# A decoder step with a mixture of experts: two expert weight loads issued earlier, and 16 matrix products without a reader ahead of the first expert block

## The reference

```python
merged = g_a * (y_a @ w_pa) + g_b * (y_b @ w_pb) + g_c * (y_c @ w_pc)
x = layer_norm(ALPHA * x + (1 + g1) * (merged @ w_o), ln1_g, ln1_b)
h2 = x * (1 + sc2) + sh2
...
scores = jax.nn.sigmoid(h @ w_router)          # group-limited top 2 of scores + bias
for e in range(N_EXPERTS):
    he = jax.nn.silu(h @ w_e_gate[e]) * (h @ w_e_up[e])
    y = y + gate[..., e:e + 1] * (he @ w_e_down[e])
x = layer_norm(ALPHA * x + (1 + g2) * y, ln2_g, ln2_b)
```

## Time and profile before

| | |
|---|---|
| median of 3 runs | 1046.58 us (1044.06 to 1046.66) |
| profiled execution | 1057.31 us, its span 1055.4 us |
| PE busy | 998.1 us (95%), 9475 matmul records |
| DVE, ACT, POOL busy | 548.5, 198.9, 254.2 us |
| granted TensorE clock, mean | 0.97 |
| HBM read, written | 201.12 MB, 16.92 MB |

### The profile page before, as it was taken

How to read it: one execution, slowest core, us unless ns; L and a number is a source line. 1 busy time by engine, 2 the same in 40 slices (tenths; PEclk the granted TensorE clock), 3 DMA queues, 4 the chain that set the end, 5 groups by cost and what they waited for, 6 DMA issues and landing times. The chain is left out here.

```text
span 1055.4 us, 23402 instructions
## 1 busy us (share of the span) xinstructions
PE 998.1 (95%) x9475; PEld 719.8 (68%) x9475; DVE 548.5 (52%) x1381; ACT 198.9 (19%) x474; POOL 254.2 (24%) x284
## 2 busy tenths in 40 slices
PE   5999999999999999899999999977999999999995
PEld 4677777557776767576777764554776777677763
DVE  1131899984457888976456815687233121011137
ACT  1110012213222323232111110111111111111104
POOL 0010002824121223123335620000211212422123
PEclk8998999999999999899999999976999999999998
DMA  9964742653605215014072336242799999899995
GB/s 307 308 139 114 240 161 82 217 206 122 238 21 164 77 31 195 20 46 126 11 191 69 120 98 271 70 189 101 306 423 416 357 410 396 347 383 396 389 277 113
DMA packets 94003, 214.98 MB, mean 204 GB/s; under 512 B 23572, under 2 KB 48407, under 8 KB 89797
## 3 DMA queue, kind: packets, MB, share of 16 engines
q1 hardware_dynamic: 78388, 186.20, 49.5%
q0 software_dynamic: 6672, 19.67, 6.2%
q10 hardware_dynamic: 8841, 7.64, 2.6%
HBM read 201.12 MB, written 16.92 MB: 207 GB/s over the span
## 5 line engine op out<-in xcount | busy, mean ns | idle before, releaser
L2120 PE MATMUL banks<-arena 128*128 128x288 f32 (+6 forms) x1774 | 427.6, 396 | 6.3 <-issue 2.5
L2120 PEld LDWEIGHTS banks<-arena 128*128 128x128 f32 (+1 forms) x1774 | 317.1, 191 | 108.9 <-issue 32.4
L2520 PE MATMUL banks<-arena 128*32 128x256 f32 x3136 | 186.7, 384 | 4.1 <-issue 2.9
L2520 PEld LDWEIGHTS banks<-arena 128*32 128x32 f32 x3136 | 131.7, 110 | 48.5 <-issue 8.1
L2048 DVE TENSOR_TENSOR arena<-arena,banks 128x128 f32<-128x128 f32 x49 | 14.1, 288 | 222.7 <-ACT arena L1353 222.5
L2542 PE MATMUL banks<-arena 128*32 128x256 f32 x1568 | 100.2, 379 | 1.5 <-issue 0.8
L1051 POOL DMA_INDIRECT expert_rows<-arena,ints x44 | 43.0, 977 | 196.9 <-ACT arena L1364 192.8
L993 POOL TENSOR_SCALAR arena<-arena 128x288 f32<-128x288 f32 x46 | 44.9, 975 | 168.2 <-ACT arena L1275 102.1
L1430 DVE SCALAR_TENSOR_TENSOR arena<-arena 128x512 f32<-128x512 f32 x120 | 82.0, 743 | 0.0
L2542 PEld LDWEIGHTS banks<-arena 128*32 128x32 f32 x1568 | 61.5, 109 | 21.7 <-issue 6.4
L2134 PE MATMUL banks<-arena 128*128 128x288 f32 x256 | 69.9, 431 | 2.7 <-DVEq L1448 2.7
(11 more groups left out here) (321 smaller groups left out, 998.4 us busy)
## 6 DMA issues: line engine op xcount, KB each, us to landing
arena<-in_w_e_gate SPq DMA_DIRECT2D x16, 2048.0 KB
arena<-in_w_e_up SPq DMA_DIRECT2D x16, 2048.0 KB
arena<-in_w_e_down SPq DMA_DIRECT2D x16, 2048.0 KB
arena<-in_w_ada SPq DMA_DIRECT2D x8, 2048.0 KB, 10.3
arena<-in_w_in SPq DMA_DIRECT2D x8, 2048.0 KB, 9.7
arena<-in_w_ada SPq DMA_DIRECT2D x8, 1024.0 KB, 11.6
arena<-in_x_prompt SPq DMA_DIRECT2D x8, 512.0 KB, 7.0
arena<-in_w_in SPq DMA_DIRECT2D x14, 256.0 KB, 8.2
```

Of the source, the lines that this page charges most:

```text
L2120: last = pe.matmul(out, a, b, start=k == 0, stop=k == len(pairs_) - 1)
L2520: last = pe.matmul(out, HG[:, g % 2, k, a:a + BLK], both_weights(i, k, c), start=k == 0, stop=k == KT - 1)
```

## The change

It does two things. First, the masks OHL, GE, OHH and the small HIS move from A_XR to a place of their own at the end of the arena (A_HOTS = A_SUMS, the arena 736 words a partition longer), so that slot 6 no longer waits for weights_up but for x1_up at 5, the last reading of R. The up weights of turn 1 are issued right behind the down weights of turn 1, in the step t == 1 of the w_o stage. Second, `unread` puts products of the identity with 256 constant columns, whose result nobody reads, into a free PSUM bank: 3 ahead of ("h2T", 4, 0), one ahead of ("cum", 3), one ahead of ("near", 3), 9 ahead of the transposes of the first gathered rows and 2 behind them.

```diff
--- before.py
+++ after.py
@@ -110,7 +110,8 @@
 A_GT = A_PT + 1024
 A_SM = A_GT + 4 * HALF + 70
 A_SUMS = A_SM + 164
-A_END = A_SUMS + 2 * 512
+A_END = A_SUMS + 2 * NT * (TS + 2 * NHI + 2)
+A_HOTS = A_SUMS
 
 A_X = A_UN
 A_WSN = A_MG
@@ -445,8 +446,8 @@
     TOTAL, NMEAN, SQUARES, RSTD2, EPSN = sm(28, 5), sm(33, 5), sm(62, 5), sm(67, 5), sm(38, 1)
     RCON = V(r0 + 1119, R_ALL)
 
-    OHL, GE, OHH = V(A_XR, 2 * NT, TS), V(A_XR + 2 * NT * TS, 2 * NT, NHI + 1), V(A_XR + 2 * NT * (TS + NHI + 1), 2 * NT, NHI)
-    SAB, HIS = V(r0 + 811, 2 * NT), V(A_XR + 2 * NT * (TS + 2 * NHI + 1), 2 * NT)
+    OHL, GE, OHH = V(A_HOTS, 2 * NT, TS), V(A_HOTS + 2 * NT * TS, 2 * NT, NHI + 1), V(A_HOTS + 2 * NT * (TS + NHI + 1), 2 * NT, NHI)
+    SAB, HIS = V(r0 + 811, 2 * NT), V(A_HOTS + 2 * NT * (TS + 2 * NHI + 1), 2 * NT)
     CMP, CMP2 = V(A_H2T, NE, NE), V(A_H2T + 256, NE, NE)
     KEY, NUM, BASE, CAP, ORD = (V(A_H2T + 512 + 16 * k, NE) for k in range(5))
 
@@ -739,7 +740,7 @@
     def room(eng, n):
 
         if n < RING:
-            eng.wait_ge(ev("weights_up"), 1)
+            eng.wait_ge(ev("x1_up"), NT)
         else:
             j, y = divmod(n - RING, 3)
             eng.wait_ge(ev("dn_full" if y == 2 else "hid_full"), FIRST[j + 1])
@@ -852,6 +853,7 @@
                 expert_weights(sp, 0, 0, 0)
                 expert_weights(sp, 0, 1, 1)
                 expert_down(sp, 1, 5)
+                expert_weights(sp, 1, 1, 4)
             if t >= 1:
                 sp.wait_ge(ev("h2_ready"), 2 * t)
                 sp.dma_start(h2_d[(t - 1) * P:t * P, :], H2[:, (t - 1) % 2, :]).then_inc(ev(f"h2_out{(t - 1) % 2}"), 16)
@@ -861,7 +863,6 @@
         sp.wait_ge(ev("h2_ready"), 2 * NT)
         sp.dma_start(h2_d[SEQ:NTOK, :], H2[0:NS, 0, :]).then_inc(ev("h2_out0"), 16)
         sp.wait_ge(ev("rows_gathered0"), 16)
-        expert_weights(sp, 1, 1, 4)
         sp.wait_ge(ev("order_known"), 1)
         for i in range(2, NE):
             e = sp.value_load(ints[0:1, I_ORD + TURNS[i]:I_ORD + TURNS[i] + 1], min_val=0, max_val=NE - 1)
@@ -2158,11 +2159,21 @@
                         last = pe.matmul(ps[NS * z:NS * z + NS, 0:256], MG[:, k, SEQ:NTOK], w[k][:, 256 * z:256 * z + 256], start=k == 0, stop=k == KT - 1)
             return last
 
+        def unread(times, cols):
+
+            pe.wait_ge(*mm.taken(("wo", 3, 1)))
+            for _ in range(times):
+                pe.matmul(mm.tile(("wo", 3, 1))[:, 0:cols], ident, con[:, 0:cols], start=True, stop=True)
+
+        fillers = {("h2T", 4, 0): (3, 256), ("cum", 3): (1, 256), ("near", 3): (1, 256)}
+
         pe.wait_ge(ev("consts"), 16)
         for key in plan:
             kind = key[0]
             if kind == "tk":
                 continue
+            if key in fillers:
+                unread(*fillers[key])
             if kind == "mod":
                 continue
             if kind == "acc":
@@ -2543,7 +2554,9 @@
                                      start=k == 0, stop=k == NJ - 1)
             last.then_inc(ev("dn_full"), 1)
 
+        unread(9, 256)
         gathered(0, 0, 16)
+        unread(2, 256)
         for b in range(NBLK + 2):
             if b < NBLK:
                 hidden(b)

```

## The result

The kernel after takes 1042.08 us in the median of 12 runs (1036.93 to 1047.35), the kernel before 1047.08 (1044.06 to 1052.73, 12 runs too, the first three of them those shown above). The two medians are 5.0 us apart; the ratio of the two sets of runs is 0.9936 (0.9918 to 0.9955), which is 6.7 us faster, 4.7 to 8.6. The forecast was 1044.1 against 1046.58, a gain of 2.5.

The account below looks back on a forecast made before the run. The prediction took TensorE to bound the expert stage, with DMA just as full, and a half clock at its start. Products 1.3 plus loads 1.2 gave 2.5 us off the median 1046.58: 1044.1, range 1041.0 to 1047.6.

Parts of the forecast that it names:

- the term for the wait ahead of block 11: Expert stage: one load less in the queue removes block 11's 1.69 us wait; 1.7 us, 1.2 for an undisturbed run.
- the up weights of turn 1: Load issued earlier, in the w_o stage: nobody waited for these weights, so by itself it gives nothing.
- the last load come 5.2 to 6.2 us forward: Queue ahead of block 11: one of eight loads gone brings the last 5.2 to 6.2 us forward.
- The one ahead of ("near", 3): Routing: this unread product finds no hole at half clock and moves the gather 0.7 us later.
- The three and the one ahead of ("cum", 3): Routing: these early unread products lie where PE idles or others wait, so they are hidden and cost nothing.
- The nine: Ahead of the first gathered rows' transposes: dense unread products take 5.6 to 6.8 us, and the clock rises during them.
- the net at block 3: First expert blocks: first block 0.95 us late, clock loss won back; net gain 1.3 us in the median run.
- rival three: Ahead of the first block: identity products do not raise the clock, or it falls again; 2.9 us slower, chance 0.07.
- block 27's wait of 1.21 moves along with PE: Expert stage: slots after block 15 fill as PE frees them, so this wait stays and moves with PE.
- rival one: Routing or expert stage: more gain than counted, by either of two branches, time 1041.7 or 1041.0; chance 0.38.
- the early products holding the clock: Routing, a branch of rival one: clock stays up, first block 1.35 us sooner, 4.9 us gained, time 1041.7.
- both waits gone: Blocks 11 and 27, a branch of rival one: no weight waits or late clock fall; 5.6 us gained, time 1041.0.

Follow-up runs that it names:

- e1: The kernel after without all 16 unread products, only the two loads issued earlier: 0.9938 of before, 1043.01 us against 1049.32.
- e5: e1's kernel with the up weights of turn 1 back behind the gather, only the gate weights of turn 2 early: 0.9941 of before.
- e7: The kernel before with only half of turn 2's down weights loaded (1 MB of 2), nothing moved: 0.9943 of before.
- e6: The kernel before with only the up weights of turn 1 issued early, no unread products: 1.0026 of before.
- e3: The kernel before, unchanged, run and profiled again: 0.9996 of before.
- e2: The kernel before plus the 16 unread products, loads not moved: 0.9969 of before.
- e8: The kernel after without the early five unread products (three, one and one); the 9 and the 2 stay: 0.9921 of before.
- e4: The kernel after, unchanged, run and profiled again: 0.9942 of before.
- e9: The kernel after with the two 0.5 MB loads of ln2's rows issued in turn 12 in place of turn 9: 0.9923 of before.
- e12: The kernel after without the early five unread products and with ln2's rows in turn 12: 0.991 of before, 1039.85 us against 1049.35.
- e10: The kernel after without any unread products and with ln2's rows in turn 12: 0.992 of before, 1040.84 us.
- e11: The kernel after without the 9 and the 2 unread products; the early five stay: 0.9953 of before.

## Why the prediction missed

The direction and the places were right, the size was not: 6.7 us came and 2.5 were forecast. The range (1041.0 to 1047.6) held the time, 1042.08.

**The step that failed** is the term for the wait ahead of block 11: "Term: 1.7, bounds 0 and 2.9 [...] I take 1.2 for an undisturbed run." The loads measured 6.5 (e1) and 6.2 (e5). The mechanism was as written: block 11 waits for weights that come late behind a full queue (the landings at e7), one load less takes the wait away (e1, e5), and the up weights of turn 1 give nothing (e6). Two things were mis-sized. The wait came from one profile, 1.69 us; in e3 it is 2.92. And I priced it as idle time alone, with the clock behind it at nothing and no reason given. In e3 the clock fell after it, and again after the wait ahead of block 27, 1.7 us each. Falls near 27 are in the profiles of e2, e3, e6 and e7 and in none of the nine with the gate weights early.

The runs agree. In the mean, time at half clock is 62 us in 29 runs of before and 57 in 11 of e1, which is worth 2.7 of the 5.6 us between the mean times; for e5 it is 2.9 of 6.5. The rest, 2.9 and 3.6, is the size of the larger wait (2.92 in e3), but the timed runs do not say where it lies. Shaving 1.7 to 1.2 because profiled executions are slow had no row behind it and went the wrong way: 6.1 of the 10.7 us that this execution lay over the median were the slow blocks. The sum also had the last load come 5.2 to 6.2 us forward; from issue to landing it gained 3.1 to 4.9, still enough. Why the clock fell after a wait in some executions and not in the first profile of before is not settled; the length of the wait does not decide it.

**The unread products** went as worked out where each step can be checked. The one ahead of ("near", 3) delays the gather at half clock (0.7 forecast; the nine start 0.68 later in after than in e8). The three and the one ahead of ("cum", 3) are hidden, and none of the five holds the clock. The nine took 6.9 us (5.6 to 6.8 forecast), the first block came 1.35 late (0.95), blocks 0 and 1 gave back 2.8 (2.97), and the net at block 3 was 1.4 to 1.5 (1.3). In the mean of the runs, too: time at half clock is 56.8 us in e1 and 51.5 in e4, worth 2.7, of which the late first block takes back 1.35. But a net of 1.3 is below what the timed runs can tell.

The clock stayed up through the eight transposes and the copies: in after, e2, e4, e8, e9 and e12 blocks 0 and 1 follow them in 7.12 us, and rival three did not happen. The Trainium skill (TensorE: Matmul & The Clock Gate, Part 4) has it that transposes do not count as busy for the clock. No fall followed them here (0.9 us of them in after), and no run tests the rule by itself.

**What I did not see** is the wait ahead of block 27. The prediction had it that "block 27's wait of 1.21 moves along with PE". The 1.21 was a low value to begin with, as e3 shows (2.29, same kernel). It was 2.85 and 2.66 in the two profiles of after, 2.08 with the loads alone, and from e1 to after about 1 of the 1.4 us that the products had won at block 3 was gone at block 48. That is no rule: e8, 4.7 us ahead of e1 at block 3, waited 2.22 and kept 4.6. e9 shows that the wait is for weights, since moving 1 MB out of their way removes it; the landings say the same, block 27 starting 0.09 us after the last landing of turn 9's up weights wherever there is a wait. Why it was longer in after is not shown; the loads of that stretch are issued at nearly the same distances behind PE. Nor is it shown why the products add 3.2 us to before and nothing measurable to the loads: without the wait (e9 and e10) the timed runs show nothing either, and the intervals are wide enough for one small gain in both places.

**The slow blocks** 28 to 32 of the profiled before were read by nobody in the forecast, and they were no part of the kernel; a comparison of the two first profiles alone would have credited the change with 11.9 us.

The chances: faster by over 0.3% had 0.38, which is rival one. Its two branches, the early products holding the clock and both waits gone, did not come; what came is more gain than counted, for a reason that was on no list. That the range held the time is thus in part luck: its lower end was rival one's 1041.0.

## What to carry over

Price a wait for a transfer in a dense stage as its idle time plus what the clock may cost after it, and take its size from more than one profile, since here it was 1.7 in one and 2.9 in the next. Where a full queue and a nearly equal engine run side by side, ask of each load what stands ahead of it that could go anywhere else. A load moved into an empty stretch was worth 6 us in timed runs; 1 MB of rows needed only at the end was worth 2.5 to 3.2 us by profile, which the timed runs are too coarse to confirm. Products without a reader raised the clock where PE would have idled anyway, and their gain in time is shown only without the loads (e2); placed inside a chain of small dependent steps at half clock they only lengthened it (e11).

## What the runs showed of the hardware

The granted clock fell to half for 3.4 us close behind waits of PE of 2.92 and 2.29 us in the middle of dense work (e3), of 2.89 in e2, 2.52 in e7 and 2.15 in e6, but not behind waits of 2.85 us in after, 2.66 in e4 or 2.08 in e1. The clock rose while PE ran products of the identity with constants: 5.6 us after the nine began in after, 3 us in e8. PE went on 0.09 us after the last landing of the load that it waited for. Two executions of one kernel (before and e3) differed by 6.1 us in five blocks, with the clock at 1.00 in both.
